# Output gates of the HGRN2 heads: from inside the head to the end of the attention ahead of it

## What is computed

```python
hn = rms_norm(h, norm1_g[l])
hq, hf, hi, hg, sq, sk, sv = jnp.split(hn @ w_in[l], split_points, axis=-1)
# HGRN2 group, 4 heads of 128: state S_t = diag(f_t) S_{t-1} + (1 - f_t) i_t^T, o_t = S_t^T q_t
f = lbh + (1.0 - lbh) * sigmoid(hf);  kf = 1.0 - f
gate = silu(hg)
y_hg = head_rms(o, norm_g) * gate
# sliding-window attention, 8 query heads of 64 in 4 pairs
y_sw = swa_group(sq, sk, sv, positions, ...)
h = h + concat([y_hg, y_sw]) @ w_out[l]
# then cross-attention to 256 memory rows, then the MLP relu(x @ up)^2 @ down
```

## Time and profile before

| | us |
|---|---|
| median of 3 runs (2804.75 to 2810.34) | 2805.92 |
| the profiled execution's own time | 2810.16 |
| its span in the profile | 2808.4 |
| PE busy | 2678.1 |
| PE weight loads busy | 2165.7 |
| DVE busy | 1757.1 |
| ACT busy | 1149.2 |
| POOL busy | 1079.7 |

### The profile page before, as it was taken

One profiled execution on the slowest core, in us unless ns is written; L12 is line 12 of the kernel. 1 busy time (PEld: TensorE's weight loads), 2 busy tenths in 40 slices (PEclk: granted clock), 3 DMA queues, 4 the chain that ended last, 5 costly groups with the idle time before them and its releaser, 6 DMA issues. The chain is left out here.

```text
span 2808.4 us, 39709 instructions
## 1 busy us (share of the span) xinstructions
PE 2678.1 (95%) x13654; PEld 2165.7 (77%) x13654; DVE 1757.1 (63%) x3012; ACT 1149.2 (41%) x2173; POOL 1079.7 (38%) x1266
## 2 busy tenths in 40 slices
PE   5999999999999997999999899999999999999999
PEld 3777777787777775887777788887888888888887
DVE  5567656766675563666565587687566454566665
ACT  4444545444454443465465532234222323322232
POOL 0322232232232222633652376657666322222222
PEclk9999999999999998999999999999999999999999
DMA  4211221131122114315522433432334764444564
GB/s 156 102 41 47 82 83 39 45 115 46 39 77 83 53 54 156 129 53 188 202 68 97 151 110 134 167 120 90 120 105 150 271 204 128 121 142 140 193 195 148
DMA packets 172557, 326.17 MB, mean 116 GB/s; under 512 B 11840, under 2 KB 77760, under 8 KB 169792
## 3 DMA queue, kind: packets, MB, share of 16 engines
q1 hardware_dynamic: 167200, 314.08, 33.3%
q10 hardware_dynamic: 5152, 9.51, 0.9%
HBM read 255.26 MB, written 68.29 MB: 115 GB/s over the span
## 5 line engine op out<-in xcount | busy, mean ns | idle before, releaser
L439 POOL TENSOR_TENSOR wlo<-raw,whi 128x256 fp32r<-128x256 f32 x612 | 504.3, 855 | 1053.7 <-ACT whi L1080 756.9
L1468 PE MATMUL bank<-hi,whi 128*128 128x512 f32 x704 | 297.3, 422 | 20.4 <-ACT vT L1053 11.1
L1471 PE MATMUL bank<-lo,whi 128*128 128x512 f32 x704 | 282.7, 402 | 5.7 <-DVE lo L1223 5.7
L3077 PE MATMUL bank<-hi,whi 128*128 128x512 f32 x896 | 276.0, 389 | 0.0
L3081 PE MATMUL bank<-hi,wlo 128*128 128x512 f32 x896 | 276.0, 389 | 0.0
L3079 PE MATMUL bank<-lo,whi 128*128 128x512 f32 x896 | 276.0, 389 | 0.0
L2592 POOL TENSOR_TENSOR wlo<-h,whi 128x256 fp32r<-128x256 f32 x160 | 127.8, 823 | 300.5 <-ACT whi L2653 300.5
L2888 DVE TENSOR_TENSOR lo<-h,hi 128x1024 fp32r<-128x1024 f32 x80 | 124.5, 1556 | 172.9 <-ACT hi L2661 172.9
L2039 PE MATMUL bank<-hi,whi 128*128 128x512 f32 x512 | 212.5, 415 | 17.9 <-POOLq L1795 6.8
L2575 POOL TENSOR_TENSOR wlo<-raw,whi 128x256 fp32r<-128x256 f32 x174 | 158.6, 936 | 148.3 <-ACT whi L2602 145.6
L2040 PE MATMUL bank<-lo,whi 128*128 128x512 f32 x512 | 202.2, 395 | 0.0
(11 more groups left out here) (379 smaller groups left out, 5966.1 us busy)
## 6 DMA issues: line engine op xcount, KB each, us to landing
h<-hidden_scratch SPq DMA_DIRECT2D x96, 512.0 KB, 4.2
raw<-w_mix SPq DMA_DIRECT2D x88, 512.0 KB, 3.2
raw<-w_cross SPq DMA_DIRECT2D x64, 512.0 KB, 3.3
raw<-w_mlp SPq DMA_DIRECT2D x64, 512.0 KB, 4.6
hidden_scratch<-hT SPq DMA_DIRECT2D x116, 256.0 KB, 2.1
h<-w_mlp SPq DMA_DIRECT2D x112, 256.0 KB, 2.9
hT<-xT SPq DMA_DIRECT2D x4, 2048.0 KB, 8.6
hT<-mixed_scratch SPq DMA_DIRECT2D x4, 2048.0 KB, 8.8
```

The costliest lines, as they stand in the source:

```text
L439: last = pool.tensor_tensor(wlo[:, i, cols], raw[:, i, cols], whi[:, i, cols].bitcast(F32), ALU.subtract)
L1468: pe.matmul(out, w, hi[:, k, :], start=k == 0, stop=False)
L1471: pe.matmul(out, w, lo[:, k, :], start=False, stop=False)
L3077: pe.matmul(down_bank(i)[:], wh[:, cols], xh[:, i % 2, :], start=K == 0, stop=False)
```

## The change

For heads 1 to 3 the two steps of the output gate leave the head and are put into the attention pair ahead of it: `out_gate h` right behind the pair's last `turn`, `out_gate_end h` behind its `att_out`. In the head, the freed places are taken by the next head's forget gate: in heads 1 and 2 `gate_start` stands where `out_gate` stood and `gate_forget` where `gate_start` stood; in head 3 `gate_start` stands where `out_gate_end` stood. Head 0 stays as it is. No instruction is added or removed, and no buffer.

```diff
         norm, root, rotate = rotated(beside)
+        gates = [[("gate_start", h + 1)], [("gate_forget", h + 1)]]
+        out = [[("out_gate", h)], [("out_gate_end", h)]]
...
         yield [("hg_o", h, 0)]
-        yield [("out_gate", h)]
+        yield from [out[0]] if h == 0 else [gates[0]] if h + 1 < HEADS else []
         yield [("hg_scores", h, 3)]
         yield [("hg_o", h, 1)]
         yield rotate
-        yield [("out_gate_end", h)]
+        yield from [out[1]] if h == 0 else [gates[0]] if h + 1 == HEADS else []
         yield [("hg_o", h, 2)]
-        yield [("gate_start", h + 1)]
+        yield gates[1] if h else gates[0]
         yield [("hg_o", h, 3)]
         yield [("hg_square", h)]
-        yield [("gate_forget", h + 1)]
+        yield from [gates[1]] if h == 0 else []
...
+    def with_out_gate(steps, h):
+        steps = list(steps)
+        last = steps.index([("turn", h * QT - 1)])
+        return steps[:last + 1] + [[("out_gate", h)]] + steps[last + 1:] + [[("out_gate_end", h)]]
...
         attention = weave(attention, gates(h)[2:], PLACES["gates"])
+        if h < HEADS:
+            attention = with_out_gate(attention, h)
```

## The result

| | median us | lowest to highest | profiled execution | span | mean granted clock |
|---|---|---|---|---|---|
| before | 2805.93 | 2804.75 to 2810.34 | 2810.16 | 2808.4 | 0.982 |
| changed | 2779.69 | 2777.02 to 2781.35 | 2777.02 | 2775.2 | 0.989 |

The changed kernel takes 0.9903 of the time, interval 0.9891 to 0.9915: 26.2 us less between the medians. Between the two profiled executions it is 33.1 us.

The account below looks back on a forecast made before the run. PE was taken as busiest but stalled by late ACT in a relay with DVE. Gains of 8.9 us in each of three blocks plus 7.0 us made 33.7: 2776.5, 2772.2 from the median, plus 2 for the clock: 2774 us, range 2765 to 2790.

Parts of the forecast that it names:

- What PE waits for: In the mixer, PE waits 15.8 us for ACT's ln of the norm total and 11.1 us for freed banks; ACT is late.
- Forget gate 2 in head 1: An earlier forget gate cuts PE's wait for the norm total from 5.26 to about 1.5 us: 3.8 us gain per block.
- Forget gate 3 in head 2: An earlier forget gate frees the bank in time, so PE's wait for it goes: 2.5 us gain per block.
- the last block's 1.8 + 1.8: In the last block, the stall behind head 1 (1.76 us) and the other freed-bank wait (1.8 us) go.
- The clock: Low-clock falls behind the removed stalls vanish: 3.8 us in each of three blocks, 3.4 us in the last.
- the first rival: The clock stays low in these places or falls at new ones, leaving 18.9 us gain, 2787 us; chance 0.16.
- a fall that turns up at another place: An estimated 2 us added to the forecast for a clock fall (1.7 us) appearing elsewhere.
- if the clock falls in head 3: One of two stated signs that the forecast is wrong; no size given.
- Output gate at the end of a pair: At the end of pair 2, ACT starts the split late: cost 1.2 us per block in the first three, bounds 0 to 2.5.
- Head 3's freed places: DVE and ACT operations removed from head 3 bring nothing; taken as 0, with 0 to 1.3 us gain possible.
- No gain: Rival: the relay is not what PE waits for, giving 2806 to 2809 us; chance 0.07.
- take its wait along: Rival: at the end of pair 2 ACT waits for DVE's addition, slower from 5.2 us on, 2810 to 2815; chance 0.05.

Follow-up runs that it names:

- e1: Against before, only head 1's output gate moves to the end of pair 0, with head 2's forget gate pulled forward: 2787.34 us, ratio 0.9931.
- e2: Against before, only head 2's output gate moves to the end of pair 1, with head 3's forget gate pulled forward: 2789.07 us, ratio 0.9939.
- e6: The kernel before, with only the norm's root step of the next block moved from the start of pair 1 to its end: 2805.84 us, ratio 1.0.
- e5: Against before, output gates of heads 1 and 2 move to the pair ahead, but the forget gate keeps its old place: 2783.72 us, ratio 0.9918.
- e4: Against before, the change made for heads 1 and 2 only, head 3 left as before: 2772.54 us, ratio 0.9881.
- e3: Against before, only head 3's output gate moves to the end of pair 2, heads 1 and 2 as before: 2815.39 us, ratio 1.0033.
- e8: The changed kernel, with DVE's copy of the state in head 3 taken ahead of three of the split's subtractions: 2774.11 us, ratio 0.9888 to before.

## Why the forecast held, point by point

**What PE waits for.** Right. e1 and e2 each take one wait away and gain 18.6 and 16.9 us. The wording "waits for the norm total" was loose, though: e6 shows that PE waits for ACT, which is late there, whatever is asked of it first.

**Forget gate 2 in head 1, 3.8 us.** Measured 3.9 a block: 15.8 less 4.1, in three blocks. e5 splits it in 3.0 and 0.9.

**Forget gate 3 in head 2, 2.5 us, and the last block's 1.8 + 1.8.** All 11.1 us went.

**The clock, 14.8 us in the sum.** PE's busy time fell by 14.6 us, and the agreement is luck. By busy time x (1 - clock), the falls that the sum named cost 14.4 us before. One of them, behind the norm total of block 1, is still there (1.7 us), and two new ones came behind head 3 (1.7 us each): 9.3 us net. That is the first rival in part, and the 2 us added for "a fall that turns up at another place" stood for it. The forecast's own sign of being wrong, "if the clock falls in head 3", came up in two blocks. What brings the figure back to 14.6 are falls of before that the forecast did not name, in blocks 0 and 1:

```profile
142.90:149.70 6.80, 6.80 (x16) 0.50 0.22 78
...
395.40:398.80 3.40, 3.40 (x8) 0.51 0.38 118
```

They cost 3.4 and 1.7 us, and at the same point of the program the changed kernel has none. The first lies ahead of the first moved step (`eg`, at 166.76 us in the changed kernel), so the change can't have removed it. Ahead of and behind the mixer, near 60 and 1900 us, two stretches differ by 1.4 us one way and 1.5 us the other. As the falls of one execution are not those of another, a gain read between two executions carries such parts: e4, whose median is 7.1 us lower, has a PE busy time 1.3 us higher in its profiled execution.

**Output gate at the end of a pair, 1.2 us a block.** In three blocks PE's waits grew by 3 x 1.15 us for `st` and 0.2 us for `lo`, 3.7 us against 3.6 in the sum. The number is right and its parts are not. The split is 0.98 us late, near the 1.2 costed, with ACT's own wait at 0.57 us. But 0.38 us of any delay was covered, and the state's copy was left out: it stands on DVE behind the split, came to lie beside POOL's subtraction and took 0.53 us more. 0.98 - 0.38 + 0.53 = 1.13 us. PE pays it at `st`, ahead of the last `lo` where the forecast looked for it.

Two costs came on top that the term did not hold: 1.4 us for `st` in the last block and the 3.4 us of clock behind head 3. Together that is some 8.5 us in a profiled execution, and e3 and e4 price head 3 at 9.5 and 7.1 us by the medians. e8, with this copy moved alone, took 3.1 us from the waits and 5.6 us from the median.

The Trainium skill names the likely cause. By its page "SBUF — State Buffer" (section "SBUF: two separate sides"), VectorE and GpSimd share a port pair that is an exclusive lock for a whole instruction, and a float32 copy within SBUF is one of the operations that need it. The trace agrees. The subtraction of POOL that was running when the copy started lasts until 533.52 + 0.93 = 534.45, and the copy ends at 534.53:

```profile
533.52 0.93 POOL L448 TENSOR_TENSOR wlo<-raw,whi 128x256 fp32r<-128x256 f32 x1 [15.65 <-ACT whi L1089]
```

All six slow copies of the state in the changed kernel end 0.08 to 0.09 us behind the end of the POOL operation that was running, also one of 0.47 us that started later in it. The other ten took 0.22 us; POOL was idle beside nine of them and about to end an operation beside the tenth. No run here moved POOL instead of the copy, so the lock itself was not shown.

**Head 3's freed places, 0 to 1.3 us of gain in the last block.** No gain: the last block's wait for `st` is 3.0 us for 1.6.

**The rivals.** "No gain" fell with the first row of PE's waits. As the prediction reads the Trainium skill's page "Perfetto Trace Analysis" (section "Identifying the Most-Contended Engine"), working on the engine with the highest occupancy would give no gain here, and 0.9903 was measured. That reading is narrow: the engine is PE, and what was shortened are PE's own waits. ACT did not take its wait along: 0.57 us, where 5.2 would have decided.

**The size.** The sum was 33.7 us from one profiled execution and 33.1 were measured between two. By the two accounts above this is luck as well: some 5 us of the 33.1 are falls of the clock that no term named, and they stand in for the head 3 costs that no term held (1.4 and 3.4 us). The medians differ by 26.2 us, 6.9 us less, since before's profiled execution lay 4.2 us above its median and the changed kernel's 2.7 us below. The forecast took the first of the two into account and had 2 us for the clock, and so came out 5.7 us too low (2774 for 2779.7).

## What to carry to other kernels

When the bound engine waits for a little-used one, follow the relay back to the longest wait of the helper and shorten the chain there. Moving the one consumer that is named only hands the wait to the next (e6). Where an operation is moved to an idle stretch, follow its delay to the end of the queue behind it, up to the next operation whose time depends on what another engine does then, and test each place alone: one of three here cost time. The gain of a profile pair and of the medians can differ by a quarter where clock falls come and go, so a forecast should be made against the median.

## What was not expected of the hardware

- A DVE copy of 128x128 takes 0.22 us, and up to 0.75 us when it starts beside one of POOL's tensor operations (0.74 to 0.93 us each). Over the changed kernel it is 217, 224 and 752 ns at least, in the middle and at most:

```profile
L1341 DVE COPY st<-state x16: 217/224/752, 101.9 to 1017.7; 128x128 f32<-128x128 f32 x16
```

- The same stall, 1.35 to 1.4 us at the same point of three blocks, was followed by a low clock in one block and by the full clock in the other two (0.76, 1.00 and 1.00 over 7 us).
- Falls of the clock are a matter of single executions as well: the profiled executions of before and of e3 took 2810.2 us both, while their medians are 9.5 us apart. In these two, e3 has 5.1 us more in the waits for `st` and `lo` and 3.8 us less PE busy time.
